# Hybrid decoder step: the state space scan reads x and the chunk state from PSUM, with eight operations for the state

## The chip, the core and the metric

The kernel runs on one core of a Trainium2 chip. The metric is the device time of one execution in microseconds; a run's time is the median of several executions. The engines are named as in the profile: PE (TensorE, with PEld for its weight loads), DVE (VectorE), ACT (ScalarE), POOL (GpSimd) and SP (SyncE, which issues DMAs here).

## The reference

Two layers: first a retention and gated delta layer, then a Mamba-2 state space layer, each followed by a SwiGLU feed forward part. 1,024 prompt tokens and 8 single new tokens go through. The change touches only the prompt's scan of the state space layer, for each of 4 groups of 8 heads of 64 channels:

```
def step(S, inp):
    xc, ac, bc, cc = inp                       # xc is x * dt
    acs = cumsum(ac, axis=1)
    lmat = where(causal, exp(acs[i] - acs[j]), 0)
    y = einsum(cc . bc, lmat, xc) + einsum(cc, S) * exp(acs)
    dec = exp(acs[:, -1:] - acs)
    S = S * exp(acs[:, -1]) + einsum(bc, dec, xc)
```

S has 128 states by 512 channels for a group. One decay factor per head, exp(acs[-1]), scales 64 of its columns.

## The kernel before

Every engine runs one fixed list of instructions and waits on semaphores; nothing is planned at run time. The big projections work on float32 numbers split into a high and a low part, so each 128x128 block of weights is three products, each in three pieces of 344 tokens: a *slice* is nine such matmuls (L565). PE's order for the state space layer is written out by hand in its `state_space(gr)`: slices of the group's z projections (`fill(z, 1)`, `fill(z, 2)`) are put between the steps of the scan, so that PE has work while DVE handles the scan.

The scan goes over 8 chunks of 128 tokens. For chunk c, PE issues: transposes of x and B of chunk c+1 and the product C·B (`front`, banks xt and bc, L1031 to L1035), one z slice, the product of the state with C (yc, L1047), the product of the scores with XDT (y, L1054), the product of B with XDEC (S, L1059), two z slices. The results go to two PSUM banks (`ps_core`) in turn, so that a bank must be read before the job after next can be written. yc{c} is such a job: it uses the bank of xt{c+1}.

DVE issues for chunk c: `front(c+1)`, which makes XDT (x by dt, from PSUM, L2253), then XDEC (XDT by the decay to the chunk's end, KDEC, both in SBUF, L2256), then CB (the masked C·B, L2259); the carried output yc by its decay (L2305); the state by its decay (step Sd, L2306, all in SBUF); for chunks 2, 4, 5 and 7 a sum for the new tokens (`sums8`, L2265); four operations that add the skip term (`skip`, L2297); the addition of the PSUM product to the state (L2313); the score product (`scores(c+1)`, L2273, all in SBUF); and the addition of the carried output (step acc, L2332, all in SBUF).

POOL meanwhile does the state update of the 8 new tokens, four tiles of four 128x1024 operations each (L519, L523, L526, L528), each tile released by `sums8` of the tile before, and splits weights (L492, L495) between them. ACT computes the decays and issues their row DMAs.

KDEC is a slice of `gtok`, 8 chunks by 32 heads; dt is another slice of it. LAST holds exp(acs[-1]) for each chunk and head, spread over all partitions.

Of the kernel before, what the change touches and what calls it, by code (L numbers as in the profile page):

```python
# [33 lines left out]
HPG, HD = 8, 64  # L34
# [145 lines left out]
def build(nc, a, o, book):  # L180

    ctx = ExitStack()
    with ctx:
        def sb(name, shape, dt=F32):
            return ctx.enter_context(nc.sbuf_tensor(name, shape, dt))
# [4 lines left out]
        def steps(name):  # L190
            return Steps(book, name, sem(name))
# [28 lines left out]
        gtok = sb("gtok", [P, NCH, 64])  # L220
# [4 lines left out]
        S = sb("S", [P, P])  # L225
# [26 lines left out]
        def tok(n, lo=0, hi=T):  # L252

            return work[:, n, lo:hi]
# [13 lines left out]
        def spread(ap, n):  # L268

            return ap.unsqueeze(2).to_broadcast([ap.shape[0], ap.shape[1], n])  # L270
# [7 lines left out]
        XDT = (work[:, 10, 8:520], work[:, 13, 8:520])  # L278
        XDEC = (work[:, 10, 520:1032], work[:, 13, 520:1032])
# [16 lines left out]
        LAST = (S[:, :].rearrange("p (c h) -> p c h", h=32), small[:, 88:216].rearrange("p (c h) -> p c h", h=32))  # L296
        KDEC = gtok[:, :, 0:32]
# [54 lines left out]
        ps_core = [ctx.enter_context(nc.psum_tensor(f"ps_core{i}", [P, 512], F32)) for i in range(2)]  # L352
# [37 lines left out]
        ssm_act, ssm_dve, ssm_pe, ssm_pool = steps("ssm_act"), steps("ssm_dve"), steps("ssm_pe"), steps("ssm_pool")  # L390
# [1293 lines left out]
        def _(dve):  # L1684
            v = nc.vector
# [552 lines left out]
            def state_space(gr):  # L2238
                big_, core = big_jobs["ssm"], core_jobs["ssm"]
                n = lambda s: f"{s}.{gr}"  # L2240
                me = lambda s: dve.wait_ge(*ssm_dve.value(n(s)))
                heads8 = lambda ap: ap.rearrange("p (h d) -> p h d", d=HD)
                mine = slice(8 * gr, 8 * gr + 8)
                col = lambda first, t: ssmc[:, first + 4 * gr + t:first + 4 * gr + t + 1]

                def front(c):

                    s = c % 2
                    dve.wait_ge(*ssm_pe.value(n(f"xt{c}")))
                    if c >= 2:  # L2250
                        dve.wait_ge(*ssm_pe.value(n(f"S{c - 2}")))
                    dt = gtok[:, c, 32 + 8 * gr:40 + 8 * gr]
                    v.tensor_tensor(heads8(XDT[s]), heads8(ps_core[core.part(n(f"xt{c}"))][:, :]), spread(dt, HD), ALU.mult)\  # L2253
                        .then_inc(core.sem(n(f"xt{c}")), 1)
                    dve.wait_ge(*core.read(n(f"xt{c}")))
                    v.tensor_tensor(heads8(XDEC[s]), heads8(XDT[s]), spread(KDEC[:, c, mine], HD), ALU.mult)\  # L2256
                        .then_inc(*ssm_dve.step(n(f"xdec{c}")))
                    dve.wait_ge(*ssm_act.value(n(f"bt{c}")))
                    v.tensor_tensor(CB[s], ps_core[core.part(n(f"bc{c}"))][:, P:2 * P], KEEP_UPPER, ALU.mult)\  # L2259
                        .then_inc(core.sem(n(f"bc{c}")), 1)  # L2260

                def sums8(t):

                    dve.wait_ge(*ssm_pool.value(n(f"SC{t}")))
                    v.tensor_reduce(SC8[:, 8 * t:8 * t + 8], UPDATE, mybir.AxisListType.X, ALU.add)\  # L2265
                        .then_inc(*ssm_dve.step(n(f"y8{t}")))

                def scores(c):

                    s = c % 2  # L2270
                    dve.wait_ge(*core.read(n(f"bc{c}")))
                    dve.wait_ge(*ssm_act.value(n(f"dec{c}")))
                    v.tensor_tensor(SC_TILE[s], SC_TILE[s], times(CB[s], HPG), ALU.mult)\  # L2273
                        .then_inc(*ssm_dve.step(n(f"score{c}")))
# [8 lines left out]
                if gr == 0:  # L2283
                    dve.wait_ge(*ssm_act.value("kdec"))
                    dve.wait_ge(*sc_act[1].value("decay"))
                front(0)
                scores(0)
                for c in range(NCH):
                    if c + 1 < NCH:
                        front(c + 1)  # L2290
                    state = work[:, 12, 0:512]
                    chunk = work[:, 0:4, c * P:c * P + P]

                    def skip():
                        dve.wait_ge(*ssm_pe.value(n(f"y{c}")))
                        for t in range(4):
                            ins = v.scalar_tensor_tensor(tok(t, c * P, c * P + P), tok(t, c * P, c * P + P), col(120, t),  # L2297
                                                         ps_core[core.part(n(f"y{c}"))][:, t * P:(t + 1) * P], ALU.mult, ALU.add)
                        ins.then_inc(core.sem(n(f"y{c}")), 1)

                    if c:
                        end = ECUM[c % 2]
                        dve.wait_ge(*ssm_pe.value(n(f"yc{c}")))
                        dve.wait_ge(*ssm_act.value(n(f"ec{c}")))
                        v.tensor_tensor(end, end, ps_core[core.part(n(f"yc{c}"))][:, :], ALU.mult).then_inc(core.sem(n(f"yc{c}")), 1)  # L2305
                        v.tensor_tensor(heads8(state), heads8(state), spread(LAST[c // 4][:, c % 4, mine], HD), ALU.mult)\  # L2306
                            .then_inc(*ssm_dve.step(n(f"Sd{c}")))
                        if c in (2, 4, 5, 7):
                            sums8((2, 4, 5, 7).index(c))
                        skip()  # L2310
                        me(f"Sd{c}")
                        dve.wait_ge(*ssm_pe.value(n(f"S{c}")))
                        v.tensor_tensor(state, state, ps_core[core.part(n(f"S{c}"))][:, :], ALU.add)\  # L2313
                            .then_inc(core.sem(n(f"S{c}")), 1)
                    else:
                        skip()
                        dve.wait_ge(*ssm_pe.value(n(f"S{c}")))
                        if gr:
                            dve.wait_ge(prompt_out[2], gr * 16)
                        v.tensor_copy(state, ps_core[core.part(n(f"S{c}"))][:, :]).then_inc(core.sem(n(f"S{c}")), 1)  # L2320
                    if c + 1 < NCH:
                        scores(c + 1)
                    else:
                        me("y83")
                        for t in range(4):
                            ins = v.scalar_tensor_tensor(tok(t, NP_TOK, T), tok(t, NP_TOK, T), col(120, t),
                                                         SC8[:, 8 * t:8 * t + 8], ALU.mult, ALU.add)
                        ins.then_inc(*ssm_dve.step(n("yd")))
                    if c:
                        dve.wait_ge(*core.read(n(f"y{c}")))  # L2330
                        dve.wait_ge(*core.read(n(f"yc{c}")))
                        v.tensor_tensor(chunk, chunk, end.rearrange("p (t n) -> p t n", n=P), ALU.add)\  # L2332
                            .then_inc(*ssm_dve.step(n(f"acc{c}")))
# [69 lines left out]
            for gr in range(GROUPS):  # L2403
                state_space(gr)
# [171 lines left out]
```

## Time and profile before

| what | value |
|---|---|
| median of 3 runs | 3330.63 us (3329.71 to 3331.18) |
| the profiled execution's own time | 3328.89 us |
| its span, first to last instruction | 3327.0 us |
| PE busy | 3149.1 us, 95% |
| DVE busy | 1766.7 us, 53% |
| POOL busy | 1019.0 us, 31% |
| mean granted TensorE clock | 0.985 |

The profile covers one execution. The four groups of the scan lie between 1785 and 2482 us of the span; each scan takes some 80 us, and the projections between them the rest. Busy shares are averages over the whole span. A row of the timeline gives start and length of an instruction, or of a run of the same instructions; the next instruction of DVE can start a little before the one before it has ended.

### The profile page before, as it was taken

How to read it: one execution, taken by the hardware profiler on the slowest of the kernel's cores; microseconds unless marked ns; L12 is line 12 of the kernel's file. 1: busy time of each engine (PE TensorE's matmuls, PEld its weight loads, DVE VectorE, ACT ScalarE, POOL GpSimd, SP SyncE). 2: the span in 40 equal slices, each digit the busy share in tenths (PEclk: the TensorE clock that was granted, in tenths of full speed). 3: DMA queues.
4: the chain of work that ended last, by engine and by line, in shares of the span. 5: the costliest groups of instructions: out<-in, count | busy, mean ns of one | idle time of the engine just before them, and what ended most of it. 6: DMA issues, size and time to landing. Idle time of an engine off the chain costs nothing. (4 is left out here: it accounts for less than half of the span.)

```text
span 3327.0 us, 46817 instructions
## 1 busy us (share of the span) xinstructions
PE 3149.1 (95%) x20090; PEld 3030.9 (91%) x20090; DVE 1766.7 (53%) x2023; ACT 799.6 (24%) x1176; POOL 1019.0 (31%) x528
## 2 busy tenths in 40 slices
PE   6999899998899999999989998999978999999997
PEld 5899898888799999999988897988968999999997
DVE  5344657556543333333487869678596333333335
ACT  4222414324420000000145415243253000000002
POOL 2222201111023333333234536345362333333331
PEclk9999999999899999999999999999999999999999
DMA  4121100101011111111114214131231111111111
GB/s 146 59 71 59 49 26 33 40 26 40 21 44 45 51 45 45 51 45 45 45 42 130 76 61 149 58 124 68 84 125 36 47 50 45 45 51 45 45 51 64
DMA packets 94474, 198.15 MB, mean 60 GB/s; under 512 B 21796, under 2 KB 52164, under 8 KB 94152
## 3 DMA queue, kind: packets, MB, share of 16 engines
q1 hardware_dynamic: 52384, 150.03, 13.4%
q10 hardware_dynamic: 41896, 45.23, 4.4%
q8 instruction: 159, 2.61, 0.3%
q14 instruction: 35, 0.29, 0.0%
HBM read 171.41 MB, written 19.59 MB: 57 GB/s over the span
## 5 line engine op out<-in xcount | busy, mean ns | idle before, releaser
L492 POOL CAST w_hi<-w_raw 128x1024 fp32r<-128x1024 f32 x230 | 256.5, 1115 | 2186.8 <-PE ps_set L565 1977.2
L565 PE MATMUL ps_set<-h_hi,w_hi 128*128 128x344 f32 x3648 | 804.5, 329 | 2.2 <-DVE work L2174 1.3
L565 PE MATMUL ps_set<-h_lo,w_hi 128*128 128x344 f32 x3648 | 774.3, 320 | 0.0
L565 PE MATMUL ps_set<-h_hi,w_lo 128*128 128x344 f32 x3648 | 770.4, 319 | 0.0
L565 PEld LDWEIGHTS ps_set<-h_hi,w_hi 128*128 128x128 f32 x3648 | 614.2, 189 | 28.4 <-issue 20.3
L565 PEld LDWEIGHTS ps_set<-h_lo,w_hi 128*128 128x128 f32 x3648 | 617.1, 189 | 0.0
L565 PEld LDWEIGHTS ps_set<-h_hi,w_lo 128*128 128x128 f32 x3648 | 608.8, 188 | 0.0
L495 POOL TENSOR_TENSOR w_lo<-w_raw,w_hi 128x1024 fp32r<-128x1024 f32 x230 | 600.6, 2611 | 18.4
L1819 DVE TENSOR_TENSOR x<-x,ps_set 128x1032 f32<-128x1032 f32 x160 | 196.6, 1229 | 255.7 <-PE ps_set L565 255.7
L1131 ACT ACTIVATE work<-work 128x1032 f32<-128x1032 f32 (+5 forms) x190 | 179.4, 958 | 492.2 <-DVE work L2174 448.2
L565 PE MATMUL ps_set<-y_hi,w_hi 128*128 128x344 f32 x1296 | 282.5, 326 | 8.5 <-DVE y_lo L2350 7.0
L1131 ACT ACTIVATE y_hi<-work 128x1032 fp32r<-128x1032 f32 (+1 forms) x98 | 63.5, 662 | 883.0 <-PE ps_set L565 633.3
L565 PE MATMUL ps_set<-y_lo,w_hi 128*128 128x344 f32 x1296 | 274.4, 320 | 0.0
L565 PE MATMUL ps_set<-y_hi,w_lo 128*128 128x344 f32 x1296 | 273.9, 319 | 0.0
L2174 DVE TENSOR_TENSOR work<-work,ps_set 128x1032 f32<-128x1032 f32 x44 | 54.1, 1229 | 340.8 <-PE ps_set L565 324.3
L565 PEld LDWEIGHTS ps_set<-y_hi,w_hi 128*128 128x128 f32 x1296 | 215.9, 189 | 13.4 <-issue 11.3
L565 PEld LDWEIGHTS ps_set<-y_lo,w_hi 128*128 128x128 f32 x1296 | 217.5, 189 | 0.0
L565 PEld LDWEIGHTS ps_set<-y_hi,w_lo 128*128 128x128 f32 x1296 | 216.5, 188 | 0.0
L836 PEld LDWEIGHTS ps_core<-work 128*128 128x128 f32 x1344 | 162.0, 197 | 28.7 <-issue 8.8
L836 PE MATMUL ps_core<-work 128*128 128x128 f32 x1344 | 171.8, 286 | 16.7 <-DVE work L2066 7.8
L1131 ACT ACTIVATE work<-ps_core 128x512 f32<-128x512 f32 (+3 forms) x164 | 72.8, 451 | 405.8 <-PE ps_core L836 142.7
L1131 ACT ACTIVATE work<-ps_set 128x1032 f32<-128x1032 f32 x72 | 74.2, 1030 | 296.8 <-PE ps_set L565 268.7
(229 smaller groups left out, 3650.2 us busy)
## 6 DMA issues: line engine op xcount, KB each, us to landing
w_raw<-in_w SPq DMA_DIRECT2D x230, 512.0 KB, 3.3
work<-ssm_cum_rows ACTq DMA_DIRECT2D x32, 512.0 KB, 4.0
sample<-in_ssm_state SPq DMA_DIRECT2D x16, 512.0 KB, 4.8
out_ssm_s<-sample SPq DMA_DIRECT2D x16, 512.0 KB, 2.6
x<-in_x SPq DMA_DIRECT2D x6, 688.0 KB, 14.9
work<-work ACTq DMA_DIRECT2D x16, 258.0 KB, 2.4
out_y<-x SPq DMA_DIRECT2D x6, 688.0 KB, 3.4
sample<-bc_rows SPq DMA_DIRECT2D x8, 512.0 KB, 4.9
```

What stands on the lines that cost most here:

```text
L492: return nc.gpsimd.tensor_copy(w_hi[:, k, :], w_raw[:, k, :])
L495: return nc.gpsimd.tensor_tensor(w_lo[:, k, :], w_raw[:, k, :], w_hi[:, k, :].bitcast(F32), ALU.subtract)
L565: mm = nc.tensor.matmul(out[:, g, 0:TN], w[:, slot, cols], v[:, g * TN:(g + 1) * TN], start=(start and n == 0), stop=(stop and n == 2))
L836: mm = nc.tensor.matmul(ps_core[part][:, c * P:(c + 1) * P], blk(lhs)[:, 4 * hf + c], blk(rhs)[:, 4 * hf + c], start=True, stop=True)
L1131: return nc.scalar.activation(out, in_, func, **kw)
L1819: v.tensor_tensor(grp(x[:, t, :]), grp(x[:, t, :]), big(jobs.part(job)), ALU.add).then_inc(jobs.sem(job), 1)
L2174: v.tensor_tensor(grp(tok(c)), grp(RSTD), big(jobs.part(name)), ALU.mult).then_inc(jobs.sem(name), 1)
```

## The change

- Once, before the first group, KDEC is multiplied by dt (a new 128x256 DVE operation with a wait on its own result). XDEC is then x by KDEC, and is read from the PSUM bank of xt like XDT. The wait between the two products is gone, and the bank is given back after the second product, not after the first.
- The operation Sd is removed. In the place of the addition stand eight operations, one per head, of 64 columns each: state = state * decay + PSUM product. The decay is a column of LAST, one scalar per partition.

```diff
                     dt = gtok[:, c, 32 + 8 * gr:40 + 8 * gr]
-                    v.tensor_tensor(heads8(XDT[s]), heads8(ps_core[core.part(n(f"xt{c}"))][:, :]), spread(dt, HD), ALU.mult)\
-                        .then_inc(core.sem(n(f"xt{c}")), 1)
-                    dve.wait_ge(*core.read(n(f"xt{c}")))
-                    v.tensor_tensor(heads8(XDEC[s]), heads8(XDT[s]), spread(KDEC[:, c, mine], HD), ALU.mult)\
-                        .then_inc(*ssm_dve.step(n(f"xdec{c}")))
+                    xt = heads8(ps_core[core.part(n(f"xt{c}"))][:, :])
+                    v.tensor_tensor(heads8(XDT[s]), xt, spread(dt, HD), ALU.mult)
+                    v.tensor_tensor(heads8(XDEC[s]), xt, spread(KDEC[:, c, mine], HD), ALU.mult).then_inc(core.sem(n(f"xt{c}")), 1)
...
                 if gr == 0:
                     dve.wait_ge(*ssm_act.value("kdec"))
                     dve.wait_ge(*sc_act[1].value("decay"))
+                    v.tensor_tensor(KDEC, KDEC, gtok[:, :, 32:64], ALU.mult).then_inc(*ssm_dve.step("dt_decay"))
+                    dve.wait_ge(*ssm_dve.value("dt_decay"))
...
-                        v.tensor_tensor(heads8(state), heads8(state), spread(LAST[c // 4][:, c % 4, mine], HD), ALU.mult)\
-                            .then_inc(*ssm_dve.step(n(f"Sd{c}")))
                         if c in (2, 4, 5, 7):
                             sums8((2, 4, 5, 7).index(c))
                         skip()
-                        me(f"Sd{c}")
+                        dve.wait_ge(*core.read(n(f"S{c - 1}")))
                         dve.wait_ge(*ssm_pe.value(n(f"S{c}")))
-                        v.tensor_tensor(state, state, ps_core[core.part(n(f"S{c}"))][:, :], ALU.add)\
-                            .then_inc(core.sem(n(f"S{c}")), 1)
+                        for h in range(HPG):
+                            head = slice(h * HD, h * HD + HD)
+                            ins = v.scalar_tensor_tensor(state[:, head], state[:, head],
+                                                         LAST[c // 4][:, c % 4, 8 * gr + h:8 * gr + h + 1],
+                                                         ps_core[core.part(n(f"S{c}"))][:, head], ALU.mult, ALU.add)
+                        ins.then_inc(core.sem(n(f"S{c}")), 1)
```

## Rows read from the trace of the kernel before

**Rows 1.** The page: busy time of each engine, share of the span, instructions.

```profile
PE 3149.1 (95%) x20090; PEld 3030.9 (91%) x20090; DVE 1766.7 (53%) x2023; ACT 799.6 (24%) x1176; POOL 1019.0 (31%) x528
```

**Rows 2.** Waits, 1760 to 2600 us: us in total, times, longest.

```profile
PE ps_core L1047 <- DVE work L2253: 21.4, 17, 2.6
...
PE ps_core L1054 <- DVE work L2259: 16.8, 16, 1.2
...
PE ps_set L565 <- DVE y_lo L2350: 7.0, 1, 7.0
```

**Rows 3.** Busy time in windows: group 0's scan, then the 20 us after it.

```profile
1799.49:1863.25 63.76, 52.97 (x380) 45.52 (x380) 59.71 (x77) 31.51 (x70) 42.71 (x18) 0.97 0.43 141
...
1866.00:1886.00 20.00, 20.00 (x129) 20.00 (x128) 19.91 (x16) 11.72 (x11) 9.71 (x4) 1.00 0.19 62
```

**Rows 4.** Groups of DVE instructions by form, the scans: xcount | busy us, mean ns.

```profile
L2256 DVE TENSOR_TENSOR work<-work,gtok 128x512 f32<-128x512 f32 x32 | 42.8, 1337 | 1.1
L2297 DVE SCALAR_TENSOR_TENSOR work<-work,ssmc,ps_core 128x128 f32<-128x128 f32 x128 | 35.6, 338 | 4.7 <-PE ps_core L1054 4.7
...
L2306 DVE TENSOR_TENSOR work<-work,small 128x512 f32<-128x512 f32 x16 | 22.0, 1373 | 0.0
...
L2306 DVE TENSOR_TENSOR work<-work,S 128x512 f32<-128x512 f32 x12 | 19.2, 1601 | 0.0
...
L2326 DVE SCALAR_TENSOR_TENSOR work<-work,ssmc,ssm 128x8 f32<-128x8 f32 x16 | 2.5, 220 | 0.0
```

**Rows 5.** One source line, the skip term: shortest, median, longest in ns.

```profile
L2297 DVE SCALAR_TENSOR_TENSOR work<-work,ssmc,ps_core x128: 330/337/347, 1793.2 to 2479.3; 128x128 f32<-128x128 f32 x128
```

**Rows 6.** Timeline of DVE in group 0: start us, length us, instruction.

```profile
1828.27 0.68 DVE L2253 TENSOR_TENSOR work<-ps_core,gtok 128x512 f32<-128x512 f32 x1
1828.98 0.69 DVE L2256 TENSOR_TENSOR work<-work,gtok 128x512 f32<-128x512 f32 x1
...
1841.45 2.06 DVE L2306 TENSOR_TENSOR work<-work,small 128x512 f32<-128x512 f32 x1
...
1844.56 1.11 DVE L2297 SCALAR_TENSOR_TENSOR work<-work,ssmc,ps_core 128x128 f32<-128x128 f32 x4
1845.60 0.67 DVE L2313 TENSOR_TENSOR work<-work,ps_core 128x512 f32<-128x512 f32 x1
1846.19 1.77 DVE L2273 TENSOR_TENSOR work<-work 128x1024 f32<-128x1024 f32 x1
1847.88 2.38 DVE L2332 TENSOR_TENSOR work<-work,masks 128x512 f32<-128x512 f32 x1
1850.19 0.68 DVE L2253 TENSOR_TENSOR work<-ps_core,gtok 128x512 f32<-128x512 f32 x1
```

**Rows 7.** Timeline of POOL in group 0.

```profile
1840.26 2.70 POOL L528 TENSOR_TENSOR sample<-sample 128x1024 f32<-128x1024 f32 x1
...
1844.49 2.39 POOL L495 TENSOR_TENSOR w_lo<-w_raw,w_hi 128x1024 fp32r<-128x1024 f32 x1
1846.83 2.89 POOL L519 TENSOR_TENSOR sample<-sample,ssm 128x1024 f32<-128x1024 f32 x1
```

**Rows 8.** Timeline of PE in group 0 (idle before, releaser in brackets).

```profile
1801.86 1.09 PE L1054 MATMUL ps_core<-work 128*64 128x128 f32 x16 [1.21 <-DVE work L2259]
...
1804.32 0.64 PE L565 MATMUL ps_set<-h_lo,w_hi 128*128 128x344 f32 x3
...
1809.87 1.09 PE L1054 MATMUL ps_core<-work 128*64 128x128 f32 x16
...
1850.92 1.16 PE L1047 MATMUL ps_core<-work 128*128 128x128 f32 x8 [2.62 <-DVE work L2253]
1852.82 1.88 PE L1054 MATMUL ps_core<-work 128*64 128x128 f32 x16 [0.74 <-DVE work L2259]
...
1856.92 0.64 PE L565 MATMUL ps_set<-h_lo,w_hi 128*128 128x344 f32 x3
...
1861.66 1.09 PE L1054 MATMUL ps_core<-work 128*64 128x128 f32 x16
```

## The prediction

> **What bounds the kernel now.** I read the page first: PE is busy for 95% of the span, DVE for 53% [rows 1]. A DVE operation saved is therefore worth nothing unless PE waits for it, so the waits come next. In the stretch with the scans PE sat idle 21.4 us before yc, waiting for XDT (L2253), and 16.8 us before y, waiting for CB (L2259) [rows 2]. Third, the windows: in group 0's scan DVE is busy 59.7 of 63.8 us and PE only 53.0; the 20 us after it PE is full, with projections that hide DVE's gating [rows 3]. So in the scan, and nearly only there, DVE sets the time. One row of PE shows the pace without a wait: y of chunk 1 at 1801.86, y of chunk 2 at 1809.87, 8.0 us a chunk; from y1 to y7 it is 59.8 us, where six paces (the last about 6.9, as no transposes follow) would be 46.9 [rows 8].
>
> **Why DVE is slow there.** L2256 (XDEC) takes 0.69 us in one place [rows 6] and 1337 ns in the mean; L2306 (Sd) 1373 and 1601 ns [rows 4]. All their inputs lie in SBUF. The timelines, laid beside each other, say what they wait for: Sd, started at 1841.45, ends at 1843.51, 0.55 after POOL's L528 (1840.26 + 2.70 = 1842.96); acc, started at 1847.88, ends at 1850.26, 0.54 after POOL's L519 (1846.83 + 2.89 = 1849.72) [rows 6, 7]. And L519, started at 1846.83, itself got going only when DVE's score product was done (1846.19 + 1.77 = 1847.96). The two take turns, one whole instruction each; POOL's own work is 2.2 us for L526 and L528 and 1.8 to 1.9 us for L519 and L523, worked out this way. L2297, which reads PSUM and SBUF, is 330 to 347 ns in 128 cases, whatever POOL did [rows 5].
>
> The Trainium skill (SBUF — State Buffer, Who interferes with whom) states that a DVE instruction with two SBUF inputs and a GpSimd instruction that reads SBUF lock each other out for the whole instruction, and that a DVE instruction with one SBUF input doesn't take part. The rows above agree. By a rule under which the two only shared a bandwidth, less overlap would be less waiting, and the rival "all of it arrives" below would lead.
>
> **The change, part by part** (pitch is from start to start).
> - XDT and XDEC: 0.71 (1828.27 to 1828.98, a wait on itself included) plus the mean of L2256 less the overlap of 0.08, 1.26: 1.97. After: two of L2253's form without that wait, 0.60 each (as 1845.60 to 1846.19 for the same width): 1.20. Saved 0.77, times 32: 24.6 us of DVE.
> - Sd: mean (16 x 1373 + 12 x 1601)/28 = 1471 ns, pitch 1.39; the addition 0.59 [rows 4, 6]. Together 1.98.
> - The eight operations. No row shows 64 columns. The nearest are L2297, 128 columns, four in 1.11 us: pitch (1.11 - 0.338)/3 = 0.257; and L2326, 8 columns, 220 ns: the same 0.08 shorter than its duration, 0.14 [rows 4, 6]. Eight cost between 1.12 and 2.06 us. Durations go linearly from 220 to 338, so 64 columns are 275 ns, pitch 0.195, eight 1.56. I take it. Saved 0.42, times 28: 12 us.
> - Together 36.6 us of DVE less. dt_decay, once, some 0.5 us with its wait, lies where DVE waits for the first transposes; without that cover it would cost its 0.5, or 2.7 with one wait for POOL.
> - The later release: yc now waits for the end of XDEC, not of XDT: XDT's start + 1.28 instead of + 0.68. y follows yc by 0.98, so y starts at XDT + 2.3. Before, it was the end of CB: + 1.9 with a free XDEC, + 3.1 with one that waited. Behind yc on DVE stands L2305, then all of the chunk.
> - Nothing is added to the DMA queues; ACT's end_rows wait for acc and move with it.
>
> The Trainium skill (VectorE: DVE Perf Modes, The TRN2 errata) gives 120 cycles and one per column for a source in PSUM, 184/0.96 GHz = 192 ns for 64 columns, and advises tiles of at least 512 elements; by it eight cost 1.53 us. That speaks against the split, which pays the fixed part eight times, but its size agrees with mine.
>
> **Where the saving goes: a walk through group 0.** DVE's 1.2 us per chunk cannot be taken off PE's loss (59.8 - 46.9, some 2 a chunk) directly, since the POOL instructions are still there and score and acc still take the lock. I walk with the pitches above and the rule of turns.
> - Up to y1: XDEC no longer waits; y1 comes at XDT + 2.3 instead of + 3.1. Gain 0.8.
> - y1 to y2: 8.0, PE's pace, as before.
> - y2 to y3, and the same for y4 to y5 (both after a sums8, which releases POOL's tile): after y2, L2305 0.1 later and 0.6 long, sums8 1.13, skip 1.03, eight operations 1.56: score is issued at +4.4. Before, score was issued 1.0 earlier and met L519 near its end. Now L519 runs +2.0 to +3.85, score meets L523 and waits to 5.65, ends at 6.7; L526 then has 2.2, acc waits for it and ends at 9.5. XDT at 9.4, XDEC to 10.7, y3 at 11.7. PE was ready for yc at +7.0, so it idles 3.7 us.
> - After the row with 2.62 us idle, PE's clock is low: y takes 1.88 against 1.09, and from y to the first quick slice 4.10 against 2.46 (1852.82 to 1856.92; 1801.86 to 1804.32) [rows 8], 1.6 lost. An idle of 3.7 will do the same. It comes twice in a group now, where before it came once.
> - y3 to y4 9.2 (PE's pace and the low clock, in part covered), y4 to y5 11.9, y5 to y6 11.1 (score meets L519, acc meets L523, idle under 2 us), y6 to y7 6.9, at PE's pace.
>
> Sum y2 to y6: 11.7 + 9.2 + 11.9 + 11.1 = 43.9, against 42.95 in the rows (1809.87 to 1852.82). y6 to y7: 6.9 against 8.84. y1 to y7: 58.8 against 59.8, and 0.8 before it: 1.8 us earlier. The starts are good to some 0.3 us, in favour of after, so I take 1.5. For the last group, which goes on with DVE's gating (PE waits 7.0 us for it [rows 2]) and so counts at DVE's end, the eight operations of chunk 7 lie on the path: 1.2. Sum 3 x 1.5 + 1.2 = 5.7 us. The profiled 3328.89 becomes 3323.2; the median is 1.74 above the profiled one, so **3325 us**.
>
> **Rivals.**
> - *The clock holds* at the 3.7 us idles, or they come out shorter: the two losses of 1.6 are gone, of which the walk, repeated without them, gives back 1.3 a group. Gain 2.7 to 2.8 a group, 10.5 in all: 3320. For it: the idle of 1.21 us before y1 left the clock alone. Against: 2.62 did not [rows 8].
> - *All of it arrives*: POOL's turns meet nothing, 36.6 us less: 3294. It would need score and acc to find POOL idle, and POOL is busy 42.7 of 63.8 us [rows 3].
> - *The waits all move on*: the turns lost by XDEC and Sd (32 x 0.65 + 28 x 0.79 = 42.8 us above their free lengths [rows 4]) come back at score, acc and yc, within 0.2%: 3331.
> - *Slower: the eight operations hit the next POOL turn.* If a 64-column operation has the pitch of a 128-column one, 0.257, the state takes 0.5 more a chunk; in the walk, acc and XDT come so late that the clock falls three times instead of two, y7 is 3.6 late and the gating 4.4: 3 x 3.6 + 4.4 = 15 us, 3346. It decides from a pitch of about 0.24, where the third idle passes 2.6 us. With the clock held even 0.257 gains.
>
> **How the numbers follow.** Chances: the walk 0.45, clock holds 0.20, all arrives 0.06, waits move on 0.17, slower 0.12. Differences of 0.2% (6.7 us) are about what a measurement can tell. Faster by more: clock holds, all arrives, and a third of the walk's own spread (3321 to 3329): 0.41. Slower by more 0.12, the rest, 0.47, within. The range, 3315 to 3336, leaves out the full saving and the three falls of the clock.
>
> **What would show it.** L2256 with 32 instructions of about 680 ns and no spread; the addition's line with 224 of some 275 ns at a pitch near 0.195; the mean of score (L2273 before, 1.66 us) and acc (L2332) higher than before; PE's idle before yc larger, now released by XDEC, and before y nearly gone; the granted clock in the scans no better. The prediction is wrong if score meets POOL elsewhere in its turn than I walked, since one turn is 2.2 us, more than the whole gain of a group.

## The result and the profile after

The changed kernel takes 3341.24 us (median of 6 runs, 3339.01 to 3345.67) against 3330.33 for the kernel before: ratio 1.0038, 95% interval 1.0028 to 1.0048. It is slower: the medians differ by 10.9 us, and the ratio says 0.38%, some 13 us; 3325 was predicted. The profiled execution took 3339.01 us, the shortest of the six; its span is 3337.2. The times and ratios below leave out two slow executions of over 7000 us, one of score_before_state and one of slices_moved.

The page after, its line of the engines, against [rows 1]: DVE is busy 18.6 us less, and the kernel is slower.

```profile
PE 3153.5 (94%) x20090; PEld 3035.5 (91%) x20090; DVE 1748.1 (52%) x2192; ACT 799.6 (24%) x1176; POOL 1007.4 (30%) x528
```

The groups of DVE instructions in the scans, by form, answer to [rows 4]. Each form costs what was forecast: the second product 678 ns in the mean and 674 to 686 in 32 cases, the state's operations 276 ns each (275 forecast).

```profile
L2271 DVE TENSOR_TENSOR work<-work 128x1024 f32<-128x1024 f32 x32 | 54.2, 1694 | 10.8 <-ACT work L1131 10.6
...
L2313 DVE SCALAR_TENSOR_TENSOR work<-work,small,ps_core 128x64 f32<-128x64 f32 x128 | 25.9, 276 | 2.0 <-PE ps_core L1059 2.0
L2334 DVE TENSOR_TENSOR work<-work 128x512 f32<-128x512 f32 x12 | 25.4, 2116 | 0.0
...
L2255 DVE TENSOR_TENSOR work<-ps_core,gtok 128x512 f32<-128x512 f32 x32 | 21.7, 678 | 0.0
L2334 DVE TENSOR_TENSOR work<-work,masks 128x512 f32<-128x512 f32 x16 | 19.6, 1226 | 0.0
```

L2334 is acc, 1814 and 1105 ns in the kernel before. The waits after answer to [rows 2]: PE's idle before yc has doubled, from 21.4 to 44.7 us, the idle before y is gone, and DVE waits for yc itself much longer (L2305, 25.8 + 13.9 us, where it was 6.7 + 4.3).

```profile
PE ps_core L1047 <- DVE work L2255: 44.7, 19, 3.7
...
DVE masks L2305 <- PE ps_core L1047: 25.8, 16, 2.0
...
DVE work L2305 <- PE ps_core L1047: 13.9, 12, 1.8
...
PE ps_set L565 <- DVE y_lo L2352: 7.3, 1, 7.3
```

Group 0's scan as a window, from its first yc on, as [rows 3]: DVE falls from 59.71 to 53.09 us busy, but the granted clock from 0.97 to 0.90. This is the group with the largest fall; over the same stretch it goes from 0.95 to 0.92 in groups 1 and 2 and from 0.97 to 0.92 in group 3.

```profile
1795.55:1863.29 67.74, 56.67 (x380) 49.22 (x380) 53.09 (x111) 31.36 (x70) 38.94 (x18) 0.90 0.38 132
```

Where it happens is read from DVE and POOL side by side, chunk 2 of group 0, just after a sums8 (L2263):

```profile
1805.99 1.21 DVE L2263 TENSOR_REDUCE ssm<-sample 128x8 f32<-128x1024 f32 x1
1807.12 1.12 DVE L2297 SCALAR_TENSOR_TENSOR work<-work,ssmc,ps_core 128x128 f32<-128x128 f32 x4
1808.15 1.62 DVE L2313 SCALAR_TENSOR_TENSOR work<-work,S,ps_core 128x64 f32<-128x64 f32 x8
1809.69 2.43 DVE L2271 TENSOR_TENSOR work<-work 128x1024 f32<-128x1024 f32 x1
1812.05 2.83 DVE L2334 TENSOR_TENSOR work<-work 128x512 f32<-128x512 f32 x1
1814.80 0.68 DVE L2254 TENSOR_TENSOR work<-ps_core,gtok 128x512 f32<-128x512 f32 x1
```

```profile
1807.29 1.90 POOL L519 TENSOR_TENSOR sample<-sample,ssm 128x1024 f32<-128x1024 f32 x1 [8.31 <-DVE ssm L2263]
1809.14 1.90 POOL L523 TENSOR_TENSOR sample<-sample,work 128x1024 f32<-128x1024 f32 x1
1811.12 3.21 POOL L526 TENSOR_TENSOR sample<-sample 128x1024 f32<-128x1024 f32 x1
```

Score is issued at 1809.69, 0.5 us after L519 has ended (1809.19). It waits for all of L523 (to 1811.04) and ends at 1812.12; L526, issued at 1811.12, starts when score is done; acc waits for L526 (to 1814.33) and ends at 1814.88. PE, timeline of the same stretch, ready since 1812.4, gets its yc at 1816.13:

```profile
1804.19 1.16 PE L1047 MATMUL ps_core<-work 128*128 128x128 f32 x8 [0.36 <-DVE work L2255]
1805.28 1.10 PE L1054 MATMUL ps_core<-work 128*64 128x128 f32 x16
...
1807.74 0.63 PE L565 MATMUL ps_set<-h_lo,w_hi 128*128 128x344 f32 x3
...
1816.13 2.07 PE L1047 MATMUL ps_core<-work 128*128 128x128 f32 x8 [3.69 <-DVE work L2255]
1818.14 1.98 PE L1054 MATMUL ps_core<-work 128*64 128x128 f32 x16
1820.04 1.90 PE L1059 MATMUL ps_core<-work 128*128 128x512 f32 x2
...
1822.25 0.63 PE L565 MATMUL ps_set<-h_lo,w_hi 128*128 128x344 f32 x3
```

After these 3.69 us idle yc, y and the S product are at the lower level of the clock: yc to the first quick slice takes 6.12 us against 3.55 us in the chunk before, 2.57 lost. That is one of the three dearest of ten such falls in the scans; the other seven lost 1.46 to 1.61 us, measured in the same way. The intervals between the starts of y in group 0, in us, by such rows:

| | y1-y2 | y2-y3 | y3-y4 | y4-y5 | y5-y6 | y6-y7 | y1-y7 |
|---|---|---|---|---|---|---|---|
| before | 8.0 | 10.9 | 9.3 | 10.9 | 11.8 | 8.8 | 59.8 |
| forecast walk | 8.0 | 11.7 | 9.2 | 11.9 | 11.1 | 6.9 | 58.8 |
| after | 8.6 | 12.9 | 9.6 | 12.8 | 12.8 | 8.3 | 65.0 |

Over the four groups y1 to y7 is 59.2 us in the mean before and 63.5 after: 4 x 4.3 = 17. Against it stand 2.3 us gained between y0 and y1, and 4.2 us by which y0 of group 0 came earlier (1787.84 against 1792.04), in a stretch that the change leaves alone but for dt_decay. 17.3 - 2.3 - 4.2 = 10.8; the spans differ by 10.2. The 4.2 are no gain of the change: y0 of group 0 lies anywhere from 1786.58 to 1794.99 in the fourteen profiled executions of this document.

### The profile page after: what moved, and what is told of

Read it like the earlier page. It is cut to its first block and busy times, and to the rows that moved or that the text cites. A ratio compares the mean times of both kernels' runs of the same rounds, so it can differ in the third digit from the quotient of the medians.

```text
span 3337.2 us, 46987 instructions
## 1 busy us (share of the span) xinstructions
PE 3153.5 (94%) x20090; PEld 3035.5 (91%) x20090; DVE 1748.1 (52%) x2192; ACT 799.6 (24%) x1176; POOL 1007.4 (30%) x528
## 3 DMA queue, kind: packets, MB, share of 16 engines
q1 hardware_dynamic: 52384, 150.03, 12.9%
## 5 line engine op out<-in xcount | busy, mean ns | idle before, releaser
L1131 ACT ACTIVATE y_hi<-work 128x1032 fp32r<-128x1032 f32 (+1 forms) x98 | 63.5, 662 | 882.9 <-PE ps_set L565 633.3
```

The costliest lines, as they stand in the source:

```text
L1131: return nc.scalar.activation(out, in_, func, **kw)
```

## The experiments

Ratios are to the kernel before on the same chip, with their 95% intervals. "y1-y7" is the mean of the four groups in the profiled execution.

**Which part.** The x part alone is the new front and dt_decay; the state part alone is the eight operations.

```diff
 # x_part_alone: the changed kernel, but the state as before
+v.tensor_tensor(heads8(state), heads8(state), spread(LAST..., HD), ALU.mult)
 ...skip()...
-for h in range(HPG): scalar_tensor_tensor(...)
+v.tensor_tensor(state, state, ps_core[...], ALU.add)
 # state_part_alone: the changed kernel, but front(c) as before, no dt_decay
```

Expected of x_part_alone: 

> The x part alone (dt_decay, both products from PSUM, the bank given back after the second); the state part is undone. Theory A, the eight operations push the score product one POOL instruction further, PE then idles long and its clock falls: this kernel keeps the old order of the state's steps, so it doesn't lose; between 0 and -6 us against before, low clock in the scans as in before. Theory B, the later release of the bank of xt is what PE waits for: most of the loss is here, +8 to +12 us, and L1047 waits for the second product for over 40 us. Theory C, the loss is spread over both parts: +3 to +6.

Measured: 3325.53 us, 0.9991 (0.9982 to 1.0); y1-y7 59.0. The gain of 3 us is at the edge of what the interval can tell from none.

Expected of state_part_alone: 

> The eight operations alone; XDT and XDEC as before. Theory A: the loss is here, +8 to +20 us (XDEC still waits for POOL on top), from y2 to y3 and from y4 to y5 12.5 to 13.5 us against 10.9. Theory B: no loss, -3 to +2 us. Theory C: +3 to +6.

Measured: 3358.44 us, 1.0086 (1.0072 to 1.0099); y1-y7 66.4, and y2 to y3 and y4 to y5 12.6 us in all groups. The loss is the state part's, some 29 us of it, more than the 8 to 20 of theory A; the x part takes back 16 (by the ratios) to 19 (by the medians) when both are there, though alone it gains 3. Why it is worth so much more beside the state part was not traced. In the waits of x_part_alone PE sits idle before yc for longer than in the kernel before (32.5 us against 21.4, while the 16.8 before y are gone), and the time is no worse; the later release of the bank is not the cause of the loss.

```profile
PE ps_core L1047 <- DVE work L2255: 32.5, 24, 3.2
```

**Whose turn.** POOL's tile for the new tokens is cut in both kernels: three of its four operations handle 8 columns instead of 1024, so the new tokens' state and their output are not computed.

```diff
-nc.gpsimd.tensor_tensor(S_TILE, S_TILE, UPDATE, ALU.add)
+nc.gpsimd.tensor_tensor(S_TILE[:, :, 0:1], S_TILE[:, :, 0:1], UPDATE[:, :, 0:1], ALU.add)
 # likewise L519 and L523; L528 whole
```

Expected of short_pool_before: 

> The kernel before, with three of POOL's four operations for each tile of the new tokens cut from 1024 to 8 columns (the new tokens' state and output are not computed); the fourth and the weight splits stay. It shows what POOL's turns cost before. Theory A (turns on a shared port): the all-SBUF operations of DVE get near their free lengths, and the kernel gains 8 to 20 us. If DVE's long operations have another cause, such as DMA traffic: within 3 us.

Measured: 3316.98 us, 0.9959 (0.9944 to 0.9974), three executions; y1-y7 56.8. Not all of DVE's all-SBUF operations got near their free lengths: acc did (683 and 961 ns), score went up, from 1659 to 1887 ns.

Expected of short_pool_after: 

> The changed kernel with the same cut of POOL's work. Theory A: the score product and acc no longer wait, PE's idle before yc falls under 2.6 us in most chunks, the clock falls less often, and this kernel is faster than the same cut of before (by 5 to 15 us), so that the order of the two turns round. Theory B, the late release or the fixed part of eight operations as such is the cost: it stays slower than the cut of before, by about the same 11 us.

Measured: 3299.34 us, 0.9911 (0.9893 to 0.9929), two executions; y1-y7 52.9. With POOL's tile cut the changed kernel is 17.6 us faster than the other, where with the whole tile it is 11 slower. The cut takes POOL's work away as such; that the turns are what it cost is read from the timelines above. Its idle before yc is never over 1.8 us, and acc is near its free length:

```profile
PE ps_core L1047 <- DVE work L2255: 21.2, 19, 1.8
```

```profile
L2334 DVE TENSOR_TENSOR work<-work 128x512 f32<-128x512 f32 x12 | 11.5, 961 | 0.0
...
L2334 DVE TENSOR_TENSOR work<-work,masks 128x512 f32<-128x512 f32 x16 | 10.9, 683 | 0.0
```

**The same work in another order.** Score goes ahead of the eight operations, or the eight go behind acc.

```diff
 skip()
+scores(c + 1)                 # score_before_state; chunk 0 as it was
 ...eight scalar_tensor_tensor...
-scores(c + 1)
 ...acc...
 # state_after_acc: scores(c + 1), acc, then the eight
```

Expected of score_before_state: 

> The changed kernel with the score product ahead of the eight operations; the same instructions in another order. Theory A (what POOL instruction the score product meets, and the clock, decide): score is issued 1.5 us earlier after y and meets POOL's L519 instead of L523 after a sums8; y2 to y3 and y4 to y5 fall from 12.9 and 12.8 us to 9 to 11; the chunks between them may lengthen, since DVE's work then falls on other turns; in all faster than the changed kernel by 3 to 20 us. Theory D (the eight operations cost as such: their time on DVE, or a wait of PE for the state): same work, same time, within 3 us of the changed kernel's 3341.

Measured: 3333.73 us, 1.0014 (1.0003 to 1.0025); y1-y7 60.2; y2 to y3 and y4 to y5 are 9.6 us in every group, the chunks between 11.3 to 12.8. It gives back between a half (by the medians, 4.8 us left of 10.9) and two thirds (by the ratios) of the loss, with the same instructions, and is still slower than the kernel before.

Expected of state_after_acc: 

> The changed kernel with the eight operations behind acc, so that score and acc are issued where they were in the kernel before, and the eight, which don't use the shared port, run while POOL has its turn. The bank of S is given back later, so PE waits before bc instead of before yc, in two shorter idles. Theory A: y2 to y3 and y4 to y5 9.5 to 10.5 us, fewer falls of the clock, the kernel faster than before by 5 to 20 us. Theory D: no faster than the changed kernel, or slower, as the state arrives 1.8 us later.

Measured: 3354.79 us, 1.008 (1.0066 to 1.0094); y1-y7 64.8, y2 to y3 13.0 to 14.0. The expectation of theory A failed, and the outcome is the one that theory D names, a state that arrives later. The turns went as expected (in chunk 2 of group 1 score is issued at 2021.98 and meets L519, 2021.12 to 2023.02; acc meets L523), but PE now waits 47.7 us at L1034, where the bank of S is wanted again, and a z slice and yc stand behind that wait, so DVE in its turn idles up to 3.7 us before L2305. Two short idles did not come; one long one did, at another place:

```profile
PE ps_core L1034 <- DVE work L2332: 47.7, 20, 3.9
...
DVE masks L2305 <- PE ps_core L1047: 35.7, 16, 3.7
```

**A size on either side of the turn.** Two operations of 256 columns; four heads share one decay, so the state is another one.

```diff
-for h in range(HPG):
-    head = slice(h * HD, h * HD + HD)
+for h in (0, 4):
+    head = slice(h * HD, h * HD + 4 * HD)
```

Expected of state_in_two: 

> The changed kernel with two state operations of 256 columns in the place of eight of 64 (four heads share one decay, so the state is another one). DVE's work for the state falls from 1.54 to some 0.8 us a chunk. In the changed kernel score was issued at 1809.69, 0.5 us after POOL's L519 had ended (1809.19). Theory A (the turn): score is now issued 0.75 earlier, before L519 ends, and takes its turn one instruction earlier; so y2 to y3 and y4 to y5 lose not 0.75 but 2 to 2.5 us (12.9 to about 10.6), with fewer falls of the clock, and the kernel is 20 to 35 us faster than the changed one. Theory D (only the time on DVE counts): 0.75 a chunk, y2 to y3 at 12.1, in all 8 to 20 us faster.

Measured: 3318.0 us, 0.9965 (0.9952 to 0.9979); y1-y7 56.9; y2 to y3 and y4 to y5 9.6 us, against 12.9 and 12.8. DVE saved 0.75 us in such a chunk and the chunk 3.2; some 0.9 of the 3.2 is yc back at its quick length, the rest the turn. Its DVE timeline in group 1 and POOL's beside it show why: score is issued at 2014.47, before L519 ends (2012.82 + 1.90 = 2014.72), waits a quarter of a microsecond and lets L523 go after it.

```profile
2013.69 0.86 DVE L2313 SCALAR_TENSOR_TENSOR work<-work,S,ps_core 128x256 f32<-128x256 f32 x2
2014.47 1.33 DVE L2271 TENSOR_TENSOR work<-work 128x1024 f32<-128x1024 f32 x1
2015.72 2.38 DVE L2334 TENSOR_TENSOR work<-work 128x512 f32<-128x512 f32 x1
2018.03 0.68 DVE L2254 TENSOR_TENSOR work<-ps_core,gtok 128x512 f32<-128x512 f32 x1
```

```profile
2012.82 1.90 POOL L519 TENSOR_TENSOR sample<-sample,ssm 128x1024 f32<-128x1024 f32 x1 [7.66 <-DVE ssm L2263]
2014.67 2.88 POOL L523 TENSOR_TENSOR sample<-sample,work 128x1024 f32<-128x1024 f32 x1
```

**Shorter idles on PE.** Three z slices are moved from behind S6 and S7 to the places before yc of chunks 3, 5 and 6.

```diff
-fill(z, 1)
+fill(z, 2 if c in (3, 5, 6) else 1)
...
-fill(z, 2)
+fill(z, (2, 2, 2, 2, 2, 2, 1, 0)[c])
```

Expected of slices_moved: 

> The changed kernel with three z slices moved from chunks 6 and 7 to the places before yc of chunks 3, 5 and 6. DVE's order is unchanged, so the idles there shrink from 3.7, 3.7 and 3.4 us by 1.43 each to 2.0 to 2.3; the three slices no longer stand behind S6 and S7. Theory A with the clock as a cost of its own: where DVE sets the pace the idle alone gives back only the slices taken off the end (some 3 to 4 us a group), and the clock stays high at the shorter idles, which gives another 2 to 5 a group: 15 to 30 us faster than the changed kernel. If the clock is no cost of its own: 8 to 15 us faster. If DVE's chain alone sets the pace to the end of the group: under 4 us.

Measured: 3319.61 us, 0.9974 (0.996 to 0.9987), some 21 us faster than the changed kernel; y1-y7 60.3, and from y7 to the next group's y0 133.5 us instead of 136.3. Whether its shorter idles spare PE the lower level is mixed: of eight idles of 2.29 or 2.30 us three left yc at its quick length, and after five it took 1.36 to 2.08 us. In all the clock fell seven times, against ten in the changed kernel.

```profile
1819.87 1.16 PE L1047 MATMUL ps_core<-work 128*128 128x128 f32 x8 [2.29 <-DVE work L2255]
...
2040.82 2.07 PE L1047 MATMUL ps_core<-work 128*128 128x128 f32 x8 [2.29 <-DVE work L2255]
```

Expected of x_part_slices_moved: 

> The x part alone with the same slices moved. Its idles before yc of chunks 3, 5 and 6 are 2 to 3 us; with the slices they are about 1. Expected faster than before by 8 to 20 us, as the slices taken off chunks 6 and 7 shorten the group and the clock holds. If the end of a group is set by DVE and not by PE's slices, it stays at the x part's -3 us.

Measured: 3316.86 us, 0.996 (0.9945 to 0.9976).

Expected of x_part_slices_again: 

> The same kernel as x_part_slices_moved, on the chip of this call and in more rounds: -10 to -14 us against before, ratio 0.996 to 0.997. Its profile: no idle before yc over 3 us.

Measured: 3316.82 us, 0.9959 (0.9945 to 0.9972), the same.

Expected of slices_moved_before: 

> The kernel before with the same three z slices moved. It says how much of the gain of the x part with moved slices is the slices' alone. If the parts add: ratio near 0.997 (the x part alone 0.9991, both 0.996). If the slices do nothing without the x part: 1.000.

Measured: 3316.71 us, 0.9961 (0.9947 to 0.9974). The whole gain is the slices'; on top of them the x part adds nothing that these runs can tell, so the parts do not add up as expected. The x part's 3 us may have lain in idles that the slices cover too; that is not shown.

Expected of score_first_slices: 

> The changed kernel with score ahead of the eight operations and the slices moved. Score first gave back some 6.7 us of the loss and the slices 21; PE now waits at bc for the bank of S and not at yc, ahead of the moved slices, so these cover less of it. Added up it would be 3314; as the slices stand behind the wait, I expect 3318 to 3326, not better than the x part with the slices.

Measured: 3318.66 us, 0.9966 (0.9953 to 0.998); y1-y7 60.9. As expected, no better than the other two.

The kernel before with the slices moved, or with the x part besides, beats both kernels: by some 12 to 13 us (0.996) the kernel before, and by 23 us (medians) to 26 us (0.996/1.0038 = 0.992) the changed one.

## Why the prediction was wrong

It was slower where I had put 0.47 on no change, 0.41 on a gain and 0.12 on a loss. By its own steps:

- *What bounds it, and the turns.* Right. Instructions of DVE with two inputs in SBUF and POOL's take whole turns; the cut of POOL's work turned the sign of the comparison. That is also what the Trainium skill states (SBUF — State Buffer, Who interferes with whom).
- *The prices on DVE.* Right: 276 ns and a pitch of (1.62 - 0.276)/7 = 0.192 against 0.195 forecast; XDEC 0.68. The estimate of 192 ns from the figures of the Trainium skill (VectorE: DVE Perf Modes, The TRN2 errata) is this pitch.
- *Where score and acc land.* Right in chunks 2 and 4, in order and nearly in time: score was walked to meet L523 and acc L526, PE to idle 3.7 us; the trace has 3.69.
- *Where a fall of the clock lies.* This step failed. I took the fall from one row with 2.62 us idle, where yc was still quick and y slow behind it [rows 8], and so laid the 1.6 us behind yc. The size was about right: seven of the ten falls lost 1.46 to 1.61 us, three 2.57, 2.66 and 2.87. The place was not: in all eight idles of 3.65 to 3.69 us yc itself was slow, 1.40 to 2.08 us instead of 1.16, and what comes behind yc, y on PE and L2305 on DVE, came up to 0.9 us later than walked. In group 0 that is most of what y2 to y3 and y4 to y5 are over the walk.
- *y5 to y6: "score meets L519, acc meets L523, idle under 2 us".* This step failed in all four groups, as a consequence. The slow yc5 puts all that DVE does behind it later, while POOL goes on. In group 0 score of chunk 6 is issued at 1845.10, after L523 has started (1844.83):

```profile
1838.61 2.03 PE L1047 MATMUL ps_core<-work 128*128 128x128 f32 x8 [3.67 <-DVE work L2255]
...
1844.83 1.89 POOL L523 TENSOR_TENSOR sample<-sample,work 128x1024 f32<-128x1024 f32 x1
...
1845.10 2.70 DVE L2271 TENSOR_TENSOR work<-work 128x1024 f32<-128x1024 f32 x1
```

  0.9 earlier, by which yc5 was slow (2.03 against 1.16), it would have met L519. That is worked out from the starts; no run held the clock to try it. In the other groups score comes 1.35, 1.44 and 0.21 us after the start of L523. y5 to y6 is 12.8, 12.3, 12.3 and 13.0 us instead of 11.1. The third idle is 3.35 and 3.46 us in groups 0 and 3, with a third fall; in groups 1 and 2 it is 2.30 and 2.08, and yc6 stays quick. In group 0 the starts of the next rows carry the fall on, 8.3 instead of 6.9.
- *"It comes twice in a group now, where before it came once."* Before, it came once in groups 0 and 3 only. The walk was made in group 0 and taken for three groups. In groups 1 and 2 of the kernel before the clock fell twice, after idles no longer than those that left it alone in group 0 (chunk 3 of group 0, then of group 1):

```profile
1818.42 1.16 PE L1047 MATMUL ps_core<-work 128*128 128x128 f32 x8 [1.38 <-DVE work L2253]
1820.78 1.09 PE L1054 MATMUL ps_core<-work 128*64 128x128 f32 x16 [1.20 <-DVE work L2259]
...
2024.37 1.16 PE L1047 MATMUL ps_core<-work 128*128 128x128 f32 x8 [1.38 <-DVE work L2253]
2026.72 1.71 PE L1054 MATMUL ps_core<-work 128*64 128x128 f32 x16 [1.20 <-DVE work L2259]
```

  In these two groups y6 to y7 was 7.2 us already and y1 to y7 58.5, so most of the gain that the walk found in group 0 was not there to be had.
- *The sum.* The walk gave y1 to y7 as 58.8, it is 65.0 in this group. Of the 6.2 between them 1.2 is in y2 to y3, 0.4 in y3 to y4, 0.9 in y4 to y5, 1.7 in y5 to y6, 1.4 in y6 to y7, and 0.6 in y1 to y2, where I had PE's pace and PE waited 0.36 us for the second product and DVE 1.05 for yc. The total would have been further off but for luck: the 4.2 us by which group 0 began earlier in this execution have nothing to do with the walk.
- *The rival "slower"* named three falls of the clock and 15 us. The time came near it, by another door: the rival hung them on a pitch of 0.24 or more, and the pitch was 0.192; and the third fall came in two of the four groups.
- *The rival "the clock holds"* was wrong: after 3.65 to 3.69 us it fell each time. Its 10.5 us does not come out of its own terms either: 3 x 2.8 + 1.2 is 9.6.

What the runs show as the cause: eight operations stand where one addition stood, and score, behind them, misses the end of POOL's first operation by half a microsecond; from there on it waits for a whole one, acc for the next, and PE for both. The time saved on Sd does not help here: Sd stood ahead of the sums8 that releases POOL's tile, so it moved POOL and DVE alike, while from the start of L519 to the start of score it is 2.40 us now (1807.29 to 1809.69) and was 1.46. Doing the state in two operations, or score first, brings these two chunks to 9.6 us; the first makes the kernel faster than the one before, the second leaves it 0.14% slower. From yc to the first quick slice PE lost some 19 us at the lower level in the scans of the changed kernel, in ten falls, and some 10 in those of the kernel before, in six. How much of the 11 us is the clock's own, and how much the idle that brings it down, was not separated: no run kept the idle and held the clock. slices_moved shortened both at once.

## What to carry to other kernels

An operation that takes no part in the turns still moves the ones behind it that do; where two engines take turns by whole instructions, ask first which instruction of the other engine the next all-SBUF operation will meet, and how far it is from the edge of a turn, for half a microsecond of plain work can cost three, the clock included. A slow stretch of PE after an idle is paid on top, and where it falls on a product that another engine waits for, it moves that engine against the third. Walk more than one of several like groups before you multiply: the same idles ended at different clocks here. Work that PE has to do anyway is worth most in the gap before a wait and nothing behind the last one: three slices moved gained 12 us in the kernel before, where the change lost 11.

## What the runs showed of the hardware

TensorE ran at two levels in the scans. In the changed kernel the granted clock was 1.00 (2.4 GHz) from the yc at 1804.19 on and 0.50 (1.2 GHz) after the idle of 3.69 us; it is the third number from the end:

```profile
1804.19:1807.74 3.55, 3.55 (x30) 2.78 (x31) 2.50 (x6) 2.65 (x9) 0.45 (x1) 1.00 0.26 77
1816.13:1819.00 2.87, 2.87 (x16) 2.64 (x18) 0.84 (x2) 2.76 (x9) 2.79 (x3) 0.50 0.64 198
```

At the lower level yc took 2.08 us instead of 1.16, y 1.98 instead of 1.09, and S 2.08 instead of 1.12. The length of the idle alone does not say whether the clock falls, nor from which product on: yc was slow after 1.97 us in x_part_alone and quick after 2.99 in state_in_two, where y and S were quick behind it too in three of four groups.

```profile
1821.52 2.07 PE L1047 MATMUL ps_core<-work 128*128 128x128 f32 x8 [1.97 <-DVE work L2255]
...
2050.28 1.16 PE L1047 MATMUL ps_core<-work 128*128 128x128 f32 x8 [2.99 <-DVE work L2255]
```

What else decides was not found. I had taken one row for all of them.
